# A hybrid RG-LRU, attention and ConvFFN layer: FFN norm weights multiplied in ahead of the transposes, and its split done four chunks at a time

## What is computed

```python
x = x + mixed @ w_out[layer]
hf = rms_norm(x, ffn_norm_g[layer])      # x * rsqrt(mean(x*x) + EPS) * g
up = causal_depthwise_conv(hf @ w_up[layer], ffn_conv_w[layer], ffn_conv_b[layer])
gate, val = jnp.split(up, 2, axis=-1)
x = x + (jax.nn.gelu(gate) * val) @ w_down[layer]
```

## Time and profile before

| | |
|---|---|
| median of 3 runs | 297.78 us (297.69 to 298.14) |
| the profiled execution's own time | 297.58 us |
| its span (first to last instruction) | 295.8 us |
| TensorE busy | 288.5 us, 98% of the span |
| VectorE busy | 241.3 us, 82% |
| ScalarE busy | 201.4 us, 68% |
| GpSimd busy | 11.8 us, 4% |
| granted TensorE clock | full in all 40 slices |

### The profile page before, as it was taken

One profiled execution on the slowest core, in us unless ns is written; L12 is line 12 of the kernel. 1 busy time (PEld: TensorE's weight loads), 2 busy tenths in 40 slices (PEclk: granted clock), 3 DMA queues, 4 the chain that ended last, 5 costly groups with the idle time before them and its releaser, 6 DMA issues.

```text
span 295.8 us, 4927 instructions
## 1 busy us (share of the span) xinstructions
PE 288.5 (98%) x1624; PEld 249.4 (84%) x1624; DVE 241.3 (82%) x436; ACT 201.4 (68%) x371; POOL 11.8 (4%) x29
## 2 busy tenths in 40 slices
PE   7999999999899999999999999999999999999995
PEld 7788999898688799888888888888888888888884
DVE  2998497998998767999978888888788888888864
ACT  5975498989585388888766666776766666776540
POOL 4000000900000000000000000000000000000000
PEclk9999999999999999999999999999999999999999
DMA  7999943132264701565736544463746545200003
GB/s 236 431 419 419 418 156 90 54 142 97 68 245 160 285 3 27 220 245 219 284 144 220 191 161 157 156 254 142 284 142 224 201 143 171 113 0 0 0 0 144
DMA packets 7983, 52.22 MB, mean 177 GB/s; under 512 B 896, under 2 KB 896, under 8 KB 2080
## 3 DMA queue, kind: packets, MB, share of 16 engines
q1 hardware_dynamic: 7776, 51.38, 46.5%
q0 software_dynamic: 192, 0.64, 0.6%
HBM read 50.98 MB, written 1.05 MB: 176 GB/s over the span
## 4 chain that ended last, share of the span: by engine, by line
PE 81%; ACT 8%; DVE 6%; DMA 2%; issue 2%; SPq 0%; DVEq 0%; ACTq 0%
PE bank L1278 26%; PE bank L1282 14%; PE bank L995 12%; PE bank L996 12%; PE bank L999 12%; DMA raw<-in_stream_dram 2%; ACT qk_tok L426 2%; PE bank L1250 1%; PE bank L1182 1%; DVE x_tok L987 1%; PE bank L1258 1%; DVE tanh_a L816 1%; PE bank L1215 1%; ACT w_hi L351 1%; PE bank L1060 1%
## 5 line engine op out<-in xcount | busy, mean ns | idle before, releaser
L652 DVE TENSOR_TENSOR w_lo<-raw,w_hi 128x1024 fp32r<-128x1024 f32 x93 | 111.0, 1220 | 8.4 <-ACT w_hi L351 7.7
L351 ACT ACTIVATE w_hi<-raw 128x1024 fp32r<-128x1024 f32 x87 | 89.0, 1055 | 5.6 <-PE bank L999 4.8
L1278 PE MATMUL bank<-h_both,w_hi 128*128 128x512 f32 x336 | 83.6, 391 | 0.0
L1278 PEld LDWEIGHTS bank<-h_both,w_hi 128*128 128x128 f32 x336 | 61.6, 188 | 11.8
L1282 PEld LDWEIGHTS bank<-h_both,w_lo 128*128 128x128 f32 x336 | 45.8, 190 | 3.3
L1282 PE MATMUL bank<-h_both,w_lo 128*128 128x256 f32 x336 | 46.9, 282 | 0.0
L577 ACT ACTIVATE tanh_a<-bank 128x256 f32<-128x256 f32 x44 | 16.8, 382 | 40.8 <-PE bank L1282 40.1
L996 PE MATMUL bank<-w_lo,act_hi 128*128 128x512 f32 x88 | 34.5, 392 | 0.0
L995 PE MATMUL bank<-w_hi,act_hi 128*128 128x512 f32 x88 | 34.5, 392 | 0.0
L999 PE MATMUL bank<-w_hi,act_lo 128*128 128x512 f32 x88 | 34.2, 389 | 0.0
L585 ACT ACTIVATE xc<-ygate,par 128x256 f32<-128x256 f32 x44 | 26.2, 597 | 3.2 <-DVE ygate L925 3.1
(11 more groups left out here) (162 smaller groups left out, 389.3 us busy)
## 6 DMA issues: line engine op xcount, KB each, us to landing
raw<-in_stream_dram SPq DMA_DIRECT2D x46, 1024.0 KB, 4.8
x_tok<-in_x_dram SPq DMA_DIRECT2D x2, 512.0 KB, 3.9
raw<-in_stream_dram SPq DMA_DIRECT2D x2, 512.0 KB, 6.8
out_dram<-x_tok SPq DMA_DIRECT2D x4, 256.0 KB, 2.1
p_T<-in_gates_dram POOLq DMA_DIRECT2D x1, 512.0 KB, 8.9
par<-in_params_dram POOLq DMA_DIRECT2D x1, 117.0 KB, 4.8
```

The source lines that it names most:

```text
L351: act.activation(w_hi[u % RING][:, :], raw_unit(u), ACT.Copy).then_inc(hi_done, 1)
L652: dve.tensor_tensor(w_lo[u % RING][:, :], raw_unit(u), w_hi[u % RING][:, :].bitcast(F32), ALU.subtract).then_inc(lo_done, 1)
L1278: pe.matmul(acc[:, :], whi[:, kc, :], h_both[:, kc, :, :].rearrange("p b t -> p (b t)"), start=kc == 0, stop=False)
```

## The change

The norm's weights are multiplied in while the token rows still lie across partitions, so a row of all 1024 weights is needed on every partition. GpSimd fetches it: after the last head's transpose it writes the weights' columns of `params` to a line in DRAM, element by element, waits, and loads that line into all 128 partitions of `gain_row`, which lies in the memory of `qk_tok`. VectorE multiplies each piece of `x_tok` by `gain_row` into `x_norm[m]` right after the piece's add (`f_gain`), and `f_norm` now scales `x_norm[m]` in place. With the weights in, a chunk needs no scalar of its own, and `f_part` handles four chunks (one PSUM bank, 128 x 512) in one instruction. `transpose_f(1)` fills banks 2 and 3, four chunks each, and `first_high` waits for groups of four.

```diff
--- before.py
+++ after.py
@@ -151,6 +151,8 @@
             return t[:, :, :].rearrange("p c t -> p (c t)")
 
         x_norm = [flat(decay), flat(gate_i)]
+        gain_row = flat(qk_tok)[:, 0:D_MODEL]
+        gain_line = nc.dram_tensor("gain_line", (KC, P), F32, kind="Internal").ap()
         sq_tok = flat(p_T)[:, 2560:3072]
         y_sq, a_sq = flat(xc), flat(q_T)
         y_pairs, y_sq_sum = flat(gate_r)[:, 0:512], gate_r[:, 2, :]
@@ -177,6 +179,7 @@
         x_landed = [sem(f"x_landed{m}") for m in range(TT)]
         par_landed, first_landed = sem("par_landed"), sem("first_landed")
         gates_landed = sem("gates_landed")
+        line_landed, gain_landed = sem("line_landed"), sem("gain_landed")
         out_stored = sem("out_stored")
         hi_done, lo_done, unit_used = sem("hi_done"), sem("lo_done"), sem("unit_used")
         ones_done, consts = sem("ones_done"), sem("consts")
@@ -207,7 +210,7 @@
             sem("o_done"), sem("a_sq_done"), sem("a_chunks"), sem("a_sum"), sem("a_rms_done"), sem("a_hi"))
         wout_done, x2_done, f_sq, f_rms_done, f_rec, f_normed = (
             sem("wout_done"), sem("x2_done"), sem("f_sq"), sem("f_rms_done"), sem("f_rec"), sem("f_normed"))
-        fT, fT_hi, fT_lo = sem("fT"), sem("fT_hi"), sem("fT_lo")
+        f_gained, fT, fT_hi, fT_lo = sem("f_gained"), sem("fT"), sem("fT_hi"), sem("fT_lo")
         up_base, conv_g_done, conv_v_done, gelu_done, act_ready = (
             sem("up_base"), sem("conv_g_done"), sem("conv_v_done"), sem("gelu_done"), sem("act_ready"))
         tap_g, tap_v, prod_done, act_hi_done = sem("tap_g"), sem("tap_v"), sem("prod_done"), sem("act_hi_done")
@@ -253,8 +256,11 @@
 
         def f_at(m, kc):
 
-            tile, at = (bank[kc // 4], kc % 4) if m == 0 else (bank[2 + kc % 4], kc // 4)
-            return tile[:, P * at:P * (at + 1)]
+            return bank[2 * m + kc // 4][:, P * (kc % 4):P * (kc % 4 + 1)]
+
+        def f_group(m, g):
+
+            return bank[2 * m + g][:, :].rearrange("p (k t) -> p k t", k=4)
 
         def a_at(c):
 
@@ -339,6 +345,12 @@
                 for m in range(TT):
                     part = probs[h % P_SLOTS][:, KEY_AT[m]:KEY_AT[m] + KEYS[m]]
                     pool.tensor_scalar(part, part, row_rec[:, h, m:m + 1], None, ALU.mult).then_inc(probs_scaled, 1)
+
+            pool.wait_ge(pT, HEADS)
+            pool.dma_start(gain_line, params[:, FFN_G:FFN_G + KC].rearrange("p k -> k p"),
+                           allow_slow_non_contiguous=True).then_inc(line_landed, 16)
+            pool.wait_ge(line_landed, 16)
+            pool.dma_start(gain_row, gain_line.rearrange("k p -> (k p)").partition_broadcast(P)).then_inc(gain_landed, 16)
 
 
         @block.scalar
@@ -542,33 +554,27 @@
                 act.wait_ge(f_sq, last + 1)
                 act.activation(f_rms[:, m:m + 1], f_ss[:, last:last + 1], ACT.Sqrt, bias=f_sum[:, m:m + 1],
                                scale=1.0 / D_MODEL).then_inc(f_rms_done, 1)
+                act.wait_ge(f_gained, (1, 3)[m])
                 act.wait_ge(f_rec, m + 1)
-                act.activation(x_norm[m][:, 0:F_CUT], x_tok[:, m, 0:F_CUT], ACT.Copy,
+                act.activation(x_norm[m][:, 0:F_CUT], x_norm[m][:, 0:F_CUT], ACT.Copy,
                                scale=f_rstd[:, m:m + 1]).then_inc(f_normed, 1)
 
-            def f_part(m, kc):
-                tok = slice(P * m, P * (m + 1))
-                if m == 0:
-                    act.wait_ge(fT, kc // 4 + 1)
-                else:
-                    act.wait_ge(fT, 2 + kc % 4 + 1)
-                    if kc >= 4:
-                        act.wait_ge(fT_lo, KC + kc - 4 + 1)
-                act.activation(h_hi[:, kc, tok], f_at(m, kc), ACT.Copy,
-                               scale=par[:, FFN_G + kc:FFN_G + kc + 1]).then_inc(fT_hi, 1)
+            def f_part(m, g):
+                act.wait_ge(fT, 2 * m + g + 1)
+                act.activation(h_hi[:, 4 * g:4 * g + 4, P * m:P * (m + 1)], f_group(m, g), ACT.Copy).then_inc(fT_hi, 1)
 
             his(U_FFN, U_FFN + 1)
             f_square(0)
             f_square(1)
             f_norm(0)
-            for kc in range(KC):
-                f_part(0, kc)
+            f_part(0, 0)
+            f_part(0, 1)
             f_square(2)
             f_square(3)
             f_square(4)
             f_norm(1)
-            for kc in range(KC):
-                f_part(1, kc)
+            f_part(1, 0)
+            f_part(1, 1)
 
 
             def ffn_cross(s, which, it=None):
@@ -890,33 +896,43 @@
             def f_norm(m):
                 dve.wait_ge(f_rms_done, m + 1)
                 dve.reciprocal(f_rstd[:, m:m + 1], f_rms[:, m:m + 1]).then_inc(f_rec, 1)
+                dve.wait_ge(f_gained, (2, 5)[m])
                 dve.wait_ge(f_rec, m + 1)
-                dve.tensor_scalar(x_norm[m][:, F_CUT:D_MODEL], x_tok[:, m, F_CUT:D_MODEL], f_rstd[:, m:m + 1], None,
+                dve.tensor_scalar(x_norm[m][:, F_CUT:D_MODEL], x_norm[m][:, F_CUT:D_MODEL], f_rstd[:, m:m + 1], None,
                                   ALU.mult).then_inc(f_normed, 1)
 
-            def f_part(m, kc):
-                tok = slice(P * m, P * (m + 1))
-
-                dve.wait_ge(fT_hi, 4 * (kc // 4 + 1) if m == 0 else KC + kc + 1)
-                dve.scalar_tensor_tensor(h_lo[:, kc, tok], f_at(m, kc), par[:, FFN_G + kc:FFN_G + kc + 1],
-                                         h_hi[:, kc, tok].bitcast(F32), ALU.mult, ALU.subtract).then_inc(fT_lo, 1)
+            def f_gain(i):
+
+                m, cols, _ = A_PIECES[i]
+                dve.wait_ge(x2_done, i + 1)
+                dve.tensor_tensor(x_norm[m][:, cols], x_tok[:, m, cols], gain_row[:, cols], ALU.mult).then_inc(f_gained, 1)
+
+            def f_part(m, g):
+                at, tok = slice(4 * g, 4 * g + 4), slice(P * m, P * (m + 1))
+                dve.wait_ge(fT_hi, 2 * m + g + 1)
+                dve.tensor_tensor(h_lo[:, at, tok], f_group(m, g), h_hi[:, at, tok].bitcast(F32),
+                                  ALU.subtract).then_inc(fT_lo, 1)
 
             f_add(0)
+            dve.wait_ge(gain_landed, 16)
+            f_gain(0)
             f_add(1)
             f_mean(0)
+            f_gain(1)
             f_norm(0)
             f_add(2)
-            for kc in range(KC - 2):
-                f_part(0, kc)
+            f_gain(2)
+            f_part(0, 0)
+            f_part(0, 1)
             f_add(3)
             f_mean(2)
+            f_gain(3)
             f_add(4)
-            for kc in (KC - 2, KC - 1):
-                f_part(0, kc)
             f_mean(3)
+            f_gain(4)
             f_norm(1)
-            for kc in range(KC):
-                f_part(1, kc)
+            f_part(1, 0)
+            f_part(1, 1)
 
 
             def ffn_join(s, which, it=None):
@@ -1210,7 +1226,7 @@
             def transpose_f(m):
                 pe.wait_ge(f_normed, 2 * m + 2)
 
-                for group in ((range(0, 4), range(4, 8)), ((0, 4), (1, 5), (2, 6), (3, 7)))[m]:
+                for group in (range(0, 4), range(4, 8)):
                     for k in group:
                         ins = pe.transpose(f_at(m, k), x_norm[m][:, P * k:P * (k + 1)], ident[:, :])
                     ins.then_inc(fT, 1)
@@ -1243,10 +1259,7 @@
                 out = acc[:, :].rearrange("p (b t) -> p b t", b=2)[:, :, tok]
                 pe.wait_ge(hi_done, hi_count(u))
                 for kc in range(KC):
-                    if m == 0 and kc < KC // 2:
-                        pe.wait_ge(fT_lo, KC // 2 * (which + 1))
-                    else:
-                        pe.wait_ge(fT_lo, KC * m + kc + 1)
+                    pe.wait_ge(fT_lo, 2 * m + max(kc // 4, which if m == 0 else 0) + 1)
                     pe.matmul(out, whi[:, kc, :], h_both[:, kc, :, tok], start=m == 0 and kc == 0, stop=False,
                               skip_group_check=True)
 
```

## The result

The change takes **299.7 us** (median of 15 runs, 299.1 to 302.85) against 297.95 us for the kernel before in the same session (15 runs, 297.51 to 298.89). The ratio is 1.0065, with a 95% interval of 1.0048 to 1.0082: slower, by 1.75 us. I forecast the direction of the sum (+0.45) and not its size; the time lies above my range.

The account below looks back on a forecast made before the run. Bound: delay reaching TensorE's first FFN up products reaches the end, through the norm's chain over ScalarE and VectorE. 0.56 - 0.11 = +0.45 us on the 297.78 us median gave 298.2 us; range 297.5 to 299.0.

Parts of the forecast that it names:

- the sum (+0.45): Whole kernel: 0.56 us of delay at the norm less 0.11 at the grouped products, giving +0.45 us; chance 0.6.
- Step (7): GpSimd's two DMAs after the last head's transpose: row lands near 89 us, ten before needed; sharing costs nothing.
- my ends of 2.1 and 23.7: Bounds in us for the first DMA: a small transfer's shortest landing, and 1024 pieces costing eight times the parameters' 128 rows.
- The third rival: Row lands late, so VectorE stands at piece 0's multiplication and TensorE idles: 2.4 us late, 300.6 us; chance 0.08.
- Its dearest form: Late row plus GpSimd's 0.73 us issuing grown eightfold, counted as 5.8 us more: 306 us.
- Step (1): Piece 0's multiplication between two VectorE adds, 0.69 us, delays square 1 by 0.56 us after 0.20 of slack.
- The first rival in its milder form: Instructions or hand-overs dearer: 0.05 us more at six hand-overs, +0.75 us, 298.5 us; whole rival's chance 0.2.
- Step (2): Piece 1's multiplication costs nothing, in-place scaling keeps its price; transposes of m = 0 start 0.56 us later, at 103.32.
- Step (3): Pieces 3 and 4: piece 4's add starts 0.56 us later, VectorE is free, and piece 4's multiplication hides.
- Step (4): `first_high` of m = 0 loses its 0.32 us wait; transposes of m = 1, 2.32 us behind piece 4's add, stay 0.56 late.
- (5): Products of m = 1: two hand-overs in place of eight give back 0.11 us, leaving 0.45 us of delay.
- (6): ScalarE's rounding of the next unit's weights: its parts end at 111.4, before 111.74, so nothing is late behind.

Follow-up runs that it names:

- 2: The kernel before plus the change's two transfers and VectorE's wait for the row, which nobody reads; 299.02 us, ratio 1.0020 to the kernel before.
- 5: The change with its first transfer moved to the program's start, behind the gates' weights; 299.29 us, ratio 1.0027 to the kernel before.
- 12: The kernel before plus one 1024-piece transfer, held until VectorE has split unit 19, which nobody waits for; 298.16 us, ratio 0.9989.
- 1: The change with GpSimd's first transfer held back until VectorE has split unit 20; 298.96 us, ratio 1.0039 to the kernel before.
- 4: The change with the multiplication of piece 0 moved behind the add of piece 1; 299.43 us, ratio 1.0046 to the kernel before.
- 9: Run 8 without ScalarE's two waits for the multiplied pieces; 298.17 us, ratio 1.0008 to the kernel before.
- 8: The change with fetch held back, both adds ahead of the multiplication, and waits moved ahead except ScalarE's for m = 0; 298.69 us, ratio 1.0023.
- 7: The change with fetch held back, ScalarE's added waits ahead of squares 1 and 4, VectorE's ahead of the wait for the root; 298.69 us, ratio 1.0015.
- 3: The change without multiplications, fetch and their waits, leaving only the groups of four; 298.09 us, ratio 1.0003 to the kernel before.
- 11: The change itself, unaltered, run again; 299.45 us, ratio 1.0049 to the kernel before.

## Why the prediction was wrong, step by step

**Step (7) failed**: "The two DMAs ... I cost the sharing at nothing." I asked when the row lands and whether the stream has a lead, and not what stands on VectorE while GpSimd issues. The transfers were free (in 2 they ran in full and moved nothing behind the cast; in 5 and 12 the first ran at other places without cost), the issue was not: 0.56 us on a cast that lies on the path. Undone in 1, done alone in 2, and gone again in 5 and 12. The landing was mis-sized too, without effect: 14.5 us where I took 10, between my ends of 2.1 and 23.7, and the row came with 7.5 us to spare where I had ten. The third rival, the late row, did not happen. Its dearest form is also summed too high: an issue of 0.73 us that grew eightfold would last 5.8 us, which is 5.1 more and not 5.8. It lasted 1.15.

The Trainium skill, "SBUF — State Buffer", section "SBUF: two separate sides", says that VectorE and GpSimd share a port pair as an exclusive lock: the one that "starts first gets the pair for the whole instruction". The same section of the Trainium skill warns of the case in which an fp32 copy within SBUF on VectorE keeps GpSimd from writing the descriptors of its DMA. Here it went in the other direction. By the rule the cast would end 0.69 us after the issue, at 70.63 + 1.15 + 0.69 = 72.47; it ended at 72.27. In 5 it would end at 71.06 + 0.61 + 0.69 = 72.36; it ended at 72.16. So the trace agrees with a lock, but for 0.20 us by which the cast is free before the issue's recorded end (in 5 at least 0.20). Which resource the two share, no run here shows.

**Step (1) was right in mechanism and small in size.** I had 0.56 us for square 1, and it came 0.63 later: the multiplication starts 0.85 us behind the add and not 0.79, with a wait more than the two others of its width (0.78). 4 shows the whole of it to be the place between the adds. The first rival in its milder form, 0.05 us more at a hand-over, is what happened, at two or three hand-overs and not at six.

**Step (2) failed by 0.06 us**: "The scaling in place has the same shape as before and I give it the same price." It has, but a wait more stands ahead of it: 0.26 us behind the reciprocal in place of 0.20. Together with (1) the transposes of m = 0 are 0.69 us late, where I had 0.56.

**Step (3) held**: VectorE was free for add 3 and add 4, and for their multiplications.

**Step (4) failed in a term that I held for unchanged**: "it took ... 2.32 us, all on ScalarE and VectorE and all still there". It took 111.24 - 108.59 = 2.65 us: 0.06 at the scaling, and 0.27 at the root of m = 1. 9 against 8 ties the 0.27 to an added wait on ScalarE, and 7 shows that moving both takes it away; by what mechanism stays open. The gone wait within `first_high` was right, and so was the wait that took its place (0.78 us, predicted 0.6).

**Steps (5) and (6) held**: 0.09 us back from the groups by 3 (predicted 0.11) and 0.05 in the change itself, the instructions at 0.60 and 0.69 us, the wait for the first group 0.23 us; and nothing late after 117 us.

The sum becomes 0.56 (cast) + 0.69 (m = 0) + 0.32 (m = 1) - 0.05 (behind it) = 1.52 us. The medians have 1.75 us in the first session, with an interval of 1.43 to 2.44, and 1.44 in that of 11: the sum lies between the two, and nothing beyond it is shown. The first weights' landing, 8.20 to 9.96 us over all these profiles whatever the kernel, moves a single execution by more than these differ; it is 0.62 us of the difference between the two profiles shown.

No version beats the kernel before. The nearest, 9, gives back 0.07 us at the groups and pays 0.06 us at each of the two norms for VectorE's added wait.

## What to carry to other kernels

A DMA on GpSimd's queue has a place on the engines as well as in memory: look at which VectorE instruction stands beside its issue and what hangs on that, by way of other engines' program order too, and move the issue by one instruction if it is a cast on the path. When an operation is added to an engine off the path, put it behind what the path needs, both adds here, and read the slack in hundredths: 0.20 us was all there was. Count every added semaphore wait on a chain as some 0.06 us, even if what it waits for has long been done.

## What the runs showed of the hardware

- GpSimd's element-by-element DMA issue (4 bytes each, 512 or 1024 of them) lasts 1.11 to 1.15 us, and held a 128 x 1024 fp32 to fp32r cast of VectorE, due some 0.4 us into it, in six profiles until 0.95 us after its start. A product of two SBUF tensors (1.22 us) and a scan (1.27 us for two) beside it kept their durations. The issue of one row per partition (0.61 us in 5) did not hold a cast that came 0.41 us into it; an earlier one was not tried.
- The same issue brings 48 packets on GpSimd's queue for 512 pieces and for 1024.
- That transfer of 4 KB took 10.9 (in 7) to 14.5 us in the middle of the kernel and 19.5 us beside the stream at its start.
- The root of m = 1 on ScalarE started 0.27 to 0.28 or 0.55 to 0.56 us behind the start of the last read of the accumulator, never between, with nothing to wait for that the profile shows.
